# One layer of a hybrid diffusion backbone: the output gate's silu moved into the convolution stage, the layer norm root by log and exp, and a reordered modulation stage

## The reference

```
sh1, sc1, g1, sh2, sc2, g2 = split(silu(c) @ ada_w + ada_b, 6)      # the same for c_ctx
h    = rmsnorm(x, norm1_g) * (1 + sc1) + sh1                         # modulated rows
proj = h @ w_in                                                      # 7 blocks of 512 columns
u    = proj_a * sigmoid(proj_b)                                      # convolution half
conv_out = silu(layernorm(dwconv_grid(u, taps) + bias, ln_g, ln_b))
o    = bidirectional gated scan over (q, v, forget gates), 4 heads of 128
hg   = o / rms(o) * norm_g * silu(proj_g)                            # output gate
x   += g1 * (concat(conv_out, hg) @ w_out)
x   += g2 * expert_choice_ffn(modulated rmsnorm(x))                  # 16 experts, top-k tokens
out  = rmsnorm(x, final_g)
```

## Time and profile before

| | us |
|---|---|
| median of 3 runs | 2277.78 |
| lowest, highest | 2276.29, 2279.66 |
| profiled execution, its own time | 2279.75 |
| its span in the profile | 2278.0 |
| granted TensorE clock, mean over the span | 0.973 |

### The profile page before, as it was taken

One profiled execution on the slowest core, in us unless ns is written; L12 is line 12 of the kernel. 1 busy time (PEld: TensorE's weight loads), 2 busy tenths in 40 slices (PEclk: granted clock), 3 DMA queues, 4 the chain that ended last, 5 costly groups with the idle time before them and its releaser, 6 DMA issues. The chain is left out here.

```text
span 2278.0 us, 37763 instructions
## 1 busy us (share of the span) xinstructions
PE 2149.4 (94%) x14437; PEld 1432.0 (63%) x14437; DVE 1591.4 (70%) x2204; ACT 1016.3 (45%) x1315; POOL 505.1 (22%) x538
## 2 busy tenths in 40 slices
PE   7799999999999999999975999999999999999995
PEld 3444444444878787845532777777777777777772
DVE  2749999885679787865566676666666667666666
ACT  3611002355666666555542444434444444443444
POOL 1710001012657676600004110111110111101111
PEclk9899999999999999999987999999999999999998
DMA  9341002355011211265544877778788887777886
GB/s 350 99 75 33 19 19 88 125 154 163 8 52 38 63 46 31 99 237 186 161 157 167 269 245 237 250 240 271 241 246 251 254 261 247 243 244 243 260 262 264
DMA packets 280292, 392.88 MB, mean 172 GB/s; under 512 B 101508, under 2 KB 142980, under 8 KB 279694
## 3 DMA queue, kind: packets, MB, share of 16 engines
q1 hardware_dynamic: 262062, 333.12, 44.5%
q0 software_dynamic: 16528, 56.47, 9.0%
q10 hardware_dynamic: 1616, 2.16, 0.3%
HBM read 313.44 MB, written 62.54 MB: 165 GB/s over the span
## 5 line engine op out<-in xcount | busy, mean ns | idle before, releaser
L89 PE MATMUL pgu<-xhi,mwhi 128*128 128x256 bf16 x2048 | 558.5, 273 | 0.0
L90 PE MATMUL pgu<-xlo,mwhi 128*128 128x256 bf16 x2048 | 558.4, 273 | 0.0
L91 PE MATMUL pgu<-xhi,mwlo 128*128 128x256 bf16 x2048 | 558.4, 273 | 0.0
L2483 DVE TENSOR_TENSOR mwlo<-mwst,mwhi 128x2048 bf16<-128x2048 f32 x187 | 427.0, 2284 | 0.0
L2383 ACT ACTIVATE mwhi<-mwst 128x2048 bf16<-128x2048 f32 x186 | 350.8, 1901 | 8.4 <-DMA mwst<-in_w_gate 8.4
L2391 ACT ACTIVATE thb<-pgu 128x256 f32<-128x256 f32 x128 | 49.0, 383 | 546.2 <-PE pgu L91 546.2
L676 DVE SCALAR_TENSOR_TENSOR co<-u,taps,co 128x1984 f32<-128x1984 f32 (+22 forms) x120 | 234.2, 1951 | 3.7
L2494 DVE SCALAR_TENSOR_TENSOR thb<-thb,pgu 128x256 f32<-128x256 f32 x128 | 53.8, 420 | 245.0 <-ACT thb L2391 245.0
L2318 POOL TENSOR_TENSOR mpflag<-mpflag 1x1 f32<-1x1 f32 x46 | 37.4, 813 | 819.1 <-DVE ysb L2510 552.5
L89 PEld LDWEIGHTS pgu<-xhi,mwhi 128*128 128x128 bf16 x2048 | 200.4, 98 | 24.9
L90 PEld LDWEIGHTS pgu<-xlo,mwhi 128*128 128x128 bf16 x2048 | 200.5, 98 | 24.4
(11 more groups left out here) (405 smaller groups left out, 4275.8 us busy)
## 6 DMA issues: line engine op xcount, KB each, us to landing
mwst<-in_w_gate SPq DMA_DIRECT2D x32, 2048.0 KB, 9.0
mwst<-in_w_up SPq DMA_DIRECT2D x32, 2048.0 KB, 8.1
mwst<-in_w_down SPq DMA_DIRECT2D x32, 2048.0 KB, 11.9
wst<-in_w_in SPq DMA_DIRECT2D x28, 512.0 KB, 6.1
big<-in_ada_w SPq DMA_DIRECT2D x5, 2048.0 KB, 14.1
s_rows<-row SPq DMA_DIRECT2D x16, 520.0 KB, 5.7
u<-in_ada_w SPq DMA_DIRECT2D x8, 1024.0 KB, 6.3
xt<-in_x SPq DMA_DIRECT2D x16, 512.0 KB, 4.4
```

The lines of the kernel that those rows point to most:

```text
L89: nc.tensor.matmul(out, lh, rh, start=(first and k == 0), stop=False)
L90: nc.tensor.matmul(out, lh, rl, start=False, stop=False)
L91: ins = nc.tensor.matmul(out, ll, rh, start=False, stop=(last and k == n - 1))
L2483: nc.vector.tensor_tensor(wlo[:, b, ks], wst[:, b % NS, ks], whi[:, b, ks], ALU.subtract)\
```

## The change

In the modulation stage, SP first loads the rows of groups 0 and 1 (2 context tiles and 4 latent tiles), then the four weight blocks, then the other groups; `c` and the biases are issued by ACT. `cmix` has 32 columns, and the 8 products of a block go to four column groups of 32 (k modulo 4), each to its own 32 partitions of the bank; one product of `modrow` with a 0/1 matrix `gsel` of two columns adds the four parts and turns them into columns, block by block. The later two blocks use a single column of weights. In the main loop ACT writes the f32 value `hf`, DVE copies it to bf16 `hhi`, and the rest is formed on DVE for every second step and on POOL for the others. In the convolution stage a gate job's bank is read by ACT as tanh and by DVE as `(tanh + 1) * g`, `jb` has three buffers, and the layer norm root is `exp(-0.5 * log(v + eps))` on ACT. In the heads stage `half_tanh`, `gated` and their counterparts of the last head are gone, and the load of `gT` waits for `read` of the head before.

```diff
@@ modulate_stage
-        cmix = m.sb("cmix", [P, KD, P])
+        cmix = m.sb("cmix", [P, KD, CH])
+        gsel = m.sb("gsel", [P, 2])
         def on_dve(q):
-            return q % 4 == 3
+            return q % 2 == 1
@@ sync
-                for n in range(NCH):
-                    sp.dma_start(big[:, n], ada_v[:, :, n * SEG:(n + 1) * SEG]).then_inc(ada_in[n], 16)
-                for g, (t0, n) in enumerate(groups):
+                for g in range(2):
+                    load_rows(g)
+                for n in range(NCH):
+                    sp.dma_start(big[:, n], ada_v[:, :, n * SEG:(n + 1) * SEG]).then_inc(ada_in[n], 16)
+                for g in range(2, len(groups)):
+                    load_rows(g)
@@ scalar
+                act.dma_start(cc[:, 0, :], I["c"].rearrange("a (p k) -> (a p) k", k=KD)).then_inc(c_in, 16)
+                act.dma_start(cc[:, 1, :], I["c_ctx"].rearrange("(p k) -> p k", k=KD)).then_inc(c_in, 16)
+                act.dma_start(adab, I["ada_b"][:, 0:NCH * SEG].rearrange("a (n e) -> a n e", e=SEG)).then_inc(adab_in, 16)
+                act.dma_start(adab2[:], I["ada_b"][:, 4 * SEG:6 * SEG].rearrange("a (n e) -> a n e", e=SEG)).then_inc(adab_in, 16)
-                for g in range(3):
+                for g in range(2):
                     for j in range(groups[g][1]):
                         square(g, j)
...
-                        nc.scalar.activation(K["hhi"][:, k, t0 * P:(t0 + n) * P], pt[q % 4][:, 0:n * P], ACT.Identity,
-                                             bias=modc[:, k, s:s + 1], scale=A1[:, k, s:s + 1]).then_inc(hi_ok, 1)
+                        if q >= 4:
+                            wait_lo(act, q - 4)
+                        nc.scalar.activation(hf[:, q % 4, 0:n * P], pt[q % 4][:, 0:n * P], ACT.Identity,
+                                             bias=modc[:, k, s:s + 1], scale=A1[:, k, s:s + 1]).then_inc(hf_ok, 1)
+                        if g == 0 and k >= KD - 4:
+                            square(2, k - (KD - 4))
@@ vector
+                nc.vector.tensor_reduce(gsel[:], K["ident"][:].rearrange("p (g s e) -> p s e g", g=4, s=2)[:, :, 0, :], AX.X, ALU.add)\
+                    .then_inc(c_mix, 1)
...
-                        dve.wait_ge(hi_ok, q + 1)
-                        if q >= 4:
-                            if on_dve(q):
-                                dve.wait_ge(lod_ok, q // 4)
-                            else:
-                                dve.wait_ge(lop_ok, pool_los(q - 4))
-                        nc.vector.tensor_scalar(hf[:, q % 4, 0:n * P], pt[q % 4][:, 0:n * P], A1[:, k, s:s + 1],
-                                                modc[:, k, s:s + 1], ALU.mult, ALU.add).then_inc(hf_ok, 1)
+                        dve.wait_ge(hf_ok, q + 1)
+                        nc.vector.tensor_copy(K["hhi"][:, k, t0 * P:(t0 + n) * P], hf[:, q % 4, 0:n * P]).then_inc(hi_ok, 1)
...
-                        if k < 4 and 2 <= g < len(groups) - 1:
+                        if k < 4 and 1 <= g < len(groups) - 1:
@@ tensor
+                def column_groups(n):
+                    pe.wait_ge(ada_in[n], 16)
                     for k in range(KD):
-                        nc.tensor.matmul(pm[n % 2][:], cmix[:, k, :], big[:, n, k, :], start=(k == 0), stop=False)
+                        j = k % 4
+                        last = nc.tensor.matmul(pm[n][j * CH:(j + 1) * CH], cmix[:, k, :], big[:, n, k, :],
+                                                start=(0 < k < 4), stop=(k >= 4), skip_group_check=True)
+                    last.then_inc(mod_ps, 1)
+                def columns(q):
+                    pe.wait_ge(mod_sb, q + 1)
                     for a in range(4):
                         j = 4 * q + a
-                        last = nc.tensor.transpose(pt[q][:, a * P:(a + 1) * P], modrow[:, j * P:(j + 1) * P], K["ident"][:])
+                        last = nc.tensor.matmul(pt[q][:, 2 * a:2 * a + 2], modrow[:, j * P:(j + 1) * P], gsel[:], start=True,
+                                                stop=True, skip_group_check=True)
@@ conv_stage
+    NB = 3
-        jb = m.sb("jb", [P, 2, SEG])
+        jb = m.sb("jb", [P, NB, SEG])
@@ scalar
+                    if KIND[j][0] == "g":
+                        nc.scalar.activation(jb[:, j % NB], pjob[j % 4], ACT.Tanh, scale=0.5).then_inc(gt_ok, 1)
+                        return
...
-                    nc.scalar.activation(rs[:, n % 2], pva[n % 2][:], ACT.Sqrt, bias=K["eps"][:, 0:1]).then_inc(sd_ok, 1)
+                    nc.scalar.activation(rs[:], pva[n % 2][:], ACT.Ln, bias=K["eps"][:, 0:1]).then_inc(ln_ok, 1)
+                    act.wait_ge(ln_ok, n + 1)
+                    nc.scalar.activation(rs[:], rs[:], ACT.Exp, scale=-0.5).then_inc(rs_ok, 1)
@@ vector
+                def silu(j):
+                    if KIND[j][0] != "g":
+                        return
+                    dve.wait_ge(gt_ok, gates(j))
+                    nc.vector.scalar_tensor_tensor(jb[:, j % NB], jb[:, j % NB], 1.0, pjob[j % 4], ALU.add, ALU.mult)\
+                        .then_inc(gj_ok, 1)
...
-                    dve.wait_ge(sd_ok, n + 1)
-                    nc.vector.reciprocal(rs[:, n % 2], rs[:, n % 2]).then_inc(rs_ok, 1)
@@ heads_stage
-                        wait(sp, sg_ok, h * NSEG)
+                        wait(sp, hm_ok, h * NSEG)
-                            half_tanh(r, j)
-                            last_tanh()
-                        for r, j in due(h, i, 10, prev, cur):
-                            gated(r, j)
-                            for j in range(NSEG):
-                                wait(dve, lt_ok, j + 1)
-                                nc.vector.scalar_tensor_tensor(ltg[j], ltg[j], 1.0, gT[:, seg(j)], ALU.add, ALU.mult)\
-                                    .then_inc(lg_ok, 1)
```

More of the change, by code:

```diff
@@ L118, in modulate_stage @@
         hf = m.sb("hf", [P, 4, SEG])
-        pm = [m.ps(f"pm{i}", [P, SEG]) for i in range(2)]
+        pm = [m.ps(f"pm{i}", [P, SEG]) for i in range(4)]
         pt = [m.ps(f"pt{i}", [P, SEG]) for i in range(4)]
@@ L144, in on_dve, with wait_lo @@
         def on_dve(q):
-            return q % 4 == 3
-        def pool_los(q):
-            return 3 * (q // 4) + min(3, q % 4 + 1)
+            return q % 2 == 1
+        def wait_lo(engine, q):
+            if on_dve(q):
+                engine.wait_ge(lod_ok, q // 2 + 1)
+            else:
+                engine.wait_ge(lop_ok, q // 2 + 1)
         def lo(engine, q):
@@ L261, in normed, with mod_col @@
                     nc.vector.tensor_scalar(row, row, rstd[:, g, j:j + 1], None, ALU.mult).then_inc(xn_ok, 1)
-                for n in range(NCH - 1):
-                    mod_out(n)
+                def mod_col(q):
+                    dve.wait_ge(modc_ps, q + 1)
+                    nc.vector.tensor_copy(modc[:, 4 * q:4 * q + 4, :], pt[q][:, 0:8].rearrange("p (a s) -> p a s", a=4))\
+                        .then_inc(modc_sb, 1)
                 for g in range(2):
@@ L268, in _ @@
                         normed(g, j)
-                mod_out(NCH - 1)
-                inverse(2)
-                normed(2, 0)
-                normed(2, 1)
-                for q in range(4):
-                    dve.wait_ge(modc_ps, q + 1)
-                    nc.vector.tensor_copy(modc[:, 4 * q:4 * q + 4, :],
-                                          pt[q][:].rearrange("p (a s j) -> p a s j", a=4, s=2)[:, :, :, 0])\
-                        .then_inc(modc_sb, 1)
+                for n in range(NCH):
+                    mod_out(n)
+                    if n >= 1:
+                        mod_col(n - 1)
+                mod_col(NCH - 1)
                 dve.wait_ge(modc_sb, 4)
@@ L468, in low, with gates, job_done @@
             return CW_.first[:, 1, w] if w < 2 else wlo[:, w - 2]
+        def gates(j):
+            return sum(KIND[i][0] == "g" for i in range(j + 1))
+        def job_done(engine, j):
+            if KIND[j][0] == "g":
+                engine.wait_ge(gj_ok, gates(j))
+            else:
+                engine.wait_ge(job_ok, j + 1 - gates(j))
         def to_store(j):
@@ L531, in _ @@
                 for j in range(LATE[0]):
-                    pool.wait_ge(job_ok, j + 1)
-                    pool.dma_start(*to_store(j)).then_inc(job_out[j % 2], 16)
-                for j in LATE[0] - 2, LATE[0] - 1:
-                    pool.wait_ge(job_out[j % 2], 16 * (j // 2 + 1))
+                    job_done(pool, j)
+                    pool.dma_start(*to_store(j)).then_inc(job_out[j % NB], 16)
+                for j in range(LATE[0] - NB, LATE[0]):
+                    pool.wait_ge(job_out[j % NB], 16 * (j // NB + 1))
             @block.scalar
@@ L766, in _ @@
                                 .then_inc(GW_.lo_ok, 1)
+                    for j in LN_JOBS[n][4:]:
+                        silu(j)
+                for j in REST:
+                    silu(j)
             @block.tensor
@@ L830, in _ @@
                     job(j)
```

(15 more changed lines are left out.)

126 lines of the change are left out of this document (60 added, 66 removed).

## The result

| | before | changed |
|---|---|---|
| median, us | 2277.78 (5 runs) | 2264.31 (5 runs) |
| profiled execution, its own time | 2279.75 | 2264.13 |
| its span | 2278.0 | 2262.4 |
| forecast, for a median | | 2268 (2256 to 2279) |

The changed kernel is faster: ratio 0.994, 95% interval 0.9926 to 0.9953. Timed again on another occasion it gave 2263.62 against 2275.96 (0.9953, 0.9939 to 0.9967). The direction and the range were right. The profile before ran near the slow end of its kernel (2279.75 of a median of 2277.78), the one after at its median, so the spans differ by 15.6 us and the medians by 13.5. What matters is where the 15.6 us came from, and whether the terms of the sum were the right ones.

The account below looks back on a forecast made before the run. PE was taken as the bound, busy in 94% of the span, except early in modulation and between heads. Modulation -0.4, convolution +0.4 and heads -9.5 gave -9.5: 2270.2 profiled, 2268.3 for a median, range 2256 to 2279.

Parts of the forecast that it names:

- Loads and block: Start of the modulation stage: reordered loads and column-grouped products start the main loop at 43.8, 7.6 us earlier.
- Rival 3: Modulation stage: column groups do not overlap in f32 over 512 columns, stage +10, total 2283; chance 0.09.
- The loop gives back: Main loop: DVE and POOL exclude each other, the loop takes 61 us and gives back 7.2 of 7.6.
- The price of 11.6: Main loop: a group of eight steps, half of them with scalings, takes 11.6 us plus 0.3 for the inverse root.
- Rival 1: Main loop: the exclusion does not bind, the 7.6 us lead survives, another -7, total 2261; chance 0.17.
- Convolution: Convolution stage: PE's 444 us cover the moved work; one product ahead of the last store; +0.4, bounds 0 and +2.
- Heads: Heads stage: less waiting of PE once tanh halves and DVE products leave; -9.5 us, bounds -3 and -15.
- the wait shrinks by 2.0: Between heads: each of three 2.81 us PE waits for DVE's state chain shrinks by 2.0, 6.0 us.
- rival 2: Heads: PE's chain wait becomes an equal one for ACT's logs or POOL's keys; heads -4, total 2274; chance 0.19.
- The 0.9 at each head's beginning: Start of three heads: PE's waits for POOL's keys shrink by 0.9 a head, 2.7 us, bounds 0 and 5.
- the three terms of waits and weights: Heads: 6.0 us from chain waits, 2.7 from waits for keys, less 0.5 for the last head's output weights.
- rival 4: Whole change: the named parts do nothing, lead lost in the loop, heads' PE bound met at once; 2277; chance 0.05.

Follow-up runs that it names:

- e4: The changed kernel with all eight products of a weight block in one column group of 32, one after the other: 2278.44 us, ratio 1.0009.
- e5: The changed kernel with the main loop's work divided among ACT, DVE and POOL as in the kernel before: 2262.14 us, ratio 0.9952.
- e3: The changed kernel with all 40 rests on DVE, POOL keeping the two weight splits: 2260.47 us, ratio 0.9929.
- e10: The changed kernel once more, unaltered: 2263.62 us, ratio 0.9953.
- e11: The kernel before once more, unaltered: 2278.24 us (one).
- e2: The kernel before with the changed convolution and heads stages alone, its modulation stage kept: 2270.22 us, ratio 0.9974.
- e1: The kernel before with the changed modulation stage alone: 2270.42 us, ratio 0.9975.
- e6: The changed kernel with one unused DVE product of 512 columns put back into each readout step of the heads: 2265.82 us, ratio 0.9963.

## Why the prediction was right, and where not

The total, -9.5 on the profile against -15.6, and for the medians -9.5 against -12.3 to -13.5, was near enough for the range. Term by term:

- **Loads and block** (7.6 us earlier, 41.3 to 45.7): right in kind, somewhat small. The fourth block starts at 36.27 (37.5 forecast), takes 3.31 (4), the tail 2.3 (2.3). The loop starts at 41.91 instead of 43.8, -9.5. Other runs of the same code have 40.32 to 43.70. Rival 3, no overlap, is refuted by e4: 1.92 against 7.05.
- **The loop gives back** (61 us, 50 to 65): by the prediction's own measure, up to the end of the last rest, it is 59.4 (101.3 less 41.9). So 5.6 us are given back and not 7.2, and with the earlier start 4.0 us of lead are left where 0.4 was forecast. The mechanism was right: from 50.84 on DVE is without an instruction for only 0.77 us, 18 us of its time are held, and its three groups with scalings take 12.0, 11.9 and 12.1 us where 11.9 was forecast. That these agree so well is partly luck, as two errors cancel. The price of 11.6 has one scaling for each of two pairs of steps, but the code has one in each of the first four steps; with four it is 13.0 by the prediction's own prices, before the 0.3 of the inverse root. And not all of POOL's 25 us excludes DVE: it stood still for 18. What the sum lacks is ACT in the first group, which was checked only by its total: the four squares stand together (6.3 us for four steps), four buffers don't carry DVE over them, and it waits 3.4 us there, the first step's 0.7 included. e5 prices the new division of work at 3.1 us. Rival 1 (no exclusion) is refuted by e3 and by the median of 1522 ns.
- **Convolution** (+0.4, 0 to +2): +1.75, within the bounds; e10 against e11 gives the same. The gate product ahead of the last store costs 0.77 (2.35 idle against 1.58); most of the other microsecond is the clock behind the loop, for the first ten microseconds have a mean of 0.74 where they had 0.84. e2, with the old loop, has 0.84 there and a stage only 0.8 longer. The prediction took that clock as given.
- **Heads** (-9.5, -3 to -15): -11.2 in the first pair of profiles, 3.4 to 6.8 of it by the code where e1 and e10 are compared. The step that failed is the sizing of "the wait shrinks by 2.0 ... there are three such waits. 6.0 us": in two places the wait itself shrank by 2.25, but POOL's keys took back about 1 us of it at the same place, as rival 2 said for the chain; in the third, in the last head, it did not shrink at all. The 0.9 at each head's beginning was 0.44 (0.95 to 0.51; the waits of 0.6 and 1.32 did not move). In the first pair PE's idle time in the stage fell by 5.9 us (30.4 to 24.5) where the three terms of waits and weights sum to 8.2. PE's busy time fell by 5.4 (403.6 to 398.2) with the same products: that is the clock (lost clock 20.5 and 15.4), for which the prediction had 1.3 from shorter pauses. This filled the gap, and the heads' total came near by luck; e6 shows that a pause of 2.81 us may be followed by no lower clock at all.

So the 6 us between forecast and profile are 1.9 of the loads, 1.6 of the loop, 1.7 of the heads and 2.1 of the untouched rest, less 1.35 of the convolution; and within the heads 2.3 us of waits were oversold (8.2 forecast, 5.9 measured) and 4.1 of clock undersold (1.3 and 5.4). Rival 2 was half right, rivals 1 and 3 fell, and rival 4 fails with e1 and e2, both outside noise.

## What to carry to other kernels

Before work is moved from POOL to DVE or shared between them, ask which operands it has: here DVE and POOL held each other up on SBUF, with 18 of POOL's 25 us lost to DVE, and giving DVE every rest made the loop 2.5 us shorter than sharing them (e3), while DVE's reads from PSUM stayed at 0.80 us beside POOL (e5). Look at the idle time of the engine that ends the stage before you name another as its bound: in e3 ACT waited for PE, yet from the ninth step on DVE did not wait for ACT. Count each engine's work per step of a pipelined loop and not per loop, since with four buffers the step with the most work binds, and put a product that needs another engine's copy as many steps behind it as the buffers let that engine lag. When a wait shrinks, add up all waits of the same unit before and after; and compare stages between profiles by their lost clock too, not only by a mean of two digits.

## What was not expected of the hardware

- The same heads code took 425.3 us at a mean granted clock of 0.98 and 432.6 and 433.9 at 0.95; the changed one 418.5 at 0.98 and 422.7 at 0.96. That is 4 to 9 us in a stage, nearly as much as the whole change to it.
- Eight f32 products of 32 weight columns by 512 took 1.92 us in four column groups and 7.05 in one; a single-column product of 512 took 0.95, no less than one with 128 columns (7.13 for eight, 0.89 each).
- A DVE copy of 0.42 us took 2.35 when POOL's subtraction of 1024 columns was running, with no wait shown ahead of it: such time is booked as busy.
